# The prompt's delta rule rewritten: unrolled chunks, k and v turned inside the solve, v's rows added by a second product, the gated norm taken in by token

## The reference, cut to what matters

```python
A = where(strict, (k * beta) @ k.T * decay, 0)          # per head and chunk
sol = triangular_solve(A + I, concat([v * beta, k * beta * exp(gc)]))
u, w = sol[..., :DV], sol[..., DV:]
att = (q @ k.T) * decay
v_new = u - w @ S                                       # chunk after chunk
o = (q * exp(gc)) @ S + att @ v_new
S = S * exp(g_last) + (k * exp(g_last - gc)).T @ v_new
...
o = o * rsqrt(mean(o * o, -1) + eps) * norm_g * silu(z) # the gated norm
y = o @ w_out                                           # the output projection
```

## Time and profile before

| | us |
|---|---|
| median of 3 runs | 1880.82 (1878.73 to 1885.23) |
| the profiled execution | 1885.57 |
| its span | 1883.7 |
| PE busy | 1806.7 (96%) |
| DVE busy | 1158.7 (62%) |
| ACT busy | 461.0 (24%) |
| POOL busy | 258.8 (14%) |
| mean granted clock of PE, as a share of 2.4 GHz | 0.979 |

### The profile page before, as it was taken

How to read it: one execution, slowest core, us unless ns; L and a number is a source line. 1 busy time by engine, 2 the same in 40 slices (tenths; PEclk the granted TensorE clock), 3 DMA queues, 4 the chain that set the end, 5 groups by cost and what they waited for, 6 DMA issues and landing times. The chain is left out here.

```text
span 1883.7 us, 22711 instructions
## 1 busy us (share of the span) xinstructions
PE 1806.7 (96%) x7821; PEld 1400.7 (74%) x7821; DVE 1158.7 (62%) x2236; ACT 461.0 (24%) x1069; POOL 258.8 (14%) x554
## 2 busy tenths in 40 slices
PE   7999999999898999999999999998899999999999
PEld 4777677898476777777777777776577777777767
DVE  3756577675867666666243665547766666653365
ACT  1433412652213222222001311011322222200041
POOL 0111002326032000000011100001410000001120
PEclk9999999997999999999999999999899999999999
DMA  4111111002411222224113022210122222332111
GB/s 164 68 68 67 64 34 45 1 9 92 156 45 35 78 79 79 79 79 154 62 62 124 0 109 71 99 68 24 45 90 67 86 72 81 105 112 93 68 57 51
DMA packets 44455, 138.48 MB, mean 74 GB/s; under 512 B 4792, under 2 KB 12088, under 8 KB 44224
## 3 DMA queue, kind: packets, MB, share of 16 engines
q1 hardware_dynamic: 41648, 133.42, 20.4%
...
## 5 line engine op out<-in xcount | busy, mean ns | idle before, releaser
L267 PE MATMUL bank<-z,ring 128*128 128x288 f32 x1952 | 513.4, 410 | 6.3 <-DVE z L365 3.4
L267 PEld LDWEIGHTS bank<-z,ring 128*128 128x128 f32 x1952 | 374.3, 192 | 114.7 <-issue 4.1
L267 PE MATMUL bank<-x,ring 128*128 128x288 f32 x1632 | 429.9, 411 | 10.4 <-DMA x<-in_x 6.4
L267 PEld LDWEIGHTS bank<-x,ring 128*128 128x128 f32 x1632 | 312.5, 192 | 102.8 <-issue 13.7
L1946 DVE SCALAR_TENSOR_TENSOR scratch<-scratch 128x592 f32<-128x592 f32 x176 | 146.2, 831 | 25.8 <-ACT scratch L1890 24.1
L267 PE MATMUL bank<-y,ring 128*128 128x288 f32 x616 | 156.6, 406 | 1.0 <-ACT z L2010 0.5
L267 PE MATMUL bank<-big,ring 128*128 128x288 f32 x536 | 136.5, 410 | 6.0 <-issue 5.0
L267 PEld LDWEIGHTS bank<-y,ring 128*128 128x128 f32 x616 | 116.8, 190 | 34.1 <-ACT z L2010 1.0
L267 PEld LDWEIGHTS bank<-big,ring 128*128 128x128 f32 x536 | 102.2, 192 | 36.4 <-issue 7.3
L1890 ACT ACTIVATE scratch<-scratch 128x592 f32<-128x592 f32 x88 | 69.4, 789 | 91.2 <-DVE scratch L1920 89.5
L1980 POOL COPY scratch<-scratch 128x2 f32<-128x2 f32 x88 | 26.3, 299 | 464.1 <-ACT scratch L1876 464.1
...
## 6 DMA issues: line engine op xcount, KB each, us to landing
...
```

The lines of the kernel that those rows point to most:

```text
L267: last = pe.matmul(bank[:, 0:HALF], w[:, k * P:(k + 1) * P], rhs(k), start=start and k == 0, stop=k == self.depth - 1, skip_group_check=no ...
```

## The change

The loop becomes a class `Prompt` whose four chunks are written out. Decays and T have two buffers each, so the next chunk's are made during this one; the first ones are made in the front block. There is no staging tile. k and v are turned behind the first products of the two levels, and ACT copies v scaled by beta and k scaled by the last column of the decay. ACT also takes the right side out of the bank with a scale, and PE adds v's rows by a second product into the same sum. The output is made by token: ACT copies it to OT and squares it with a sum over the columns; POOL turns the sums into 1/rms (by a power of -0.5) and multiplies; PE turns the rows back behind the next chunk's new values, and DVE gates them into BIG. The last chunk's part of that stands in the samples' block, where POOL also makes the identities. `GatedNorm` becomes `SampleNorm`, for the samples' 64 columns only, and the output projection no longer waits for a norm of the prompt.

```diff
+DEC = [scratch(9216, H, CH), scratch(0, H, CH)]
+T_INV = [scratch(5120, H, 2, CH), scratch(1024, H, 2, CH)]
+KA, YS = scratch(3072, H, 2, CH), scratch(7168, H, CH)
+KTOK, VTOK, VNEW, EG = (scratch(at, H, P) for at in (8192, 10240, 11264, 12288))
+SS, RMS = CV[:, 112:120], CV[:, 120:128]
+def first_arg_pool(pool):
+    pool.wait_ge(gc_out, H)
+    pool.wait_ge(g_dve, 7)
+    pool.wait_ge(late_in, 64)
+    pool.tensor_tensor(DEC[0], Y[:, :, 0:CH], MASKT[:].unsqueeze(1).to_broadcast([P, H, CH]), ALU.add
+                       ).then_inc(dec_arg0, 1)
+def first_decay_act(act):
+    act.wait_ge(dec_arg0, 1)
+    act.wait_ge(tok_copied, 5)
+    for h in range(H):
+        act.activation(DEC[0][:, h, :], DEC[0][:, h, :], ACT.Exp, bias=TOKS[:, 0, 0, h:h + 1])
+def normalise(pool, nth, rms, scaled):
+    pool.tensor_scalar(RMS, SS, 1.0 / P, 1e-6, ALU.mult, ALU.add).then_inc(rms, 1)
+    pool.wait_ge(rms, 2 * nth + 1)
+    pool.tensor_tensor(RMS, RMS, NEG_HALF.to_broadcast([P, H]), ALU.pow).then_inc(rms, 1)
+    pool.wait_ge(rms, 2 * nth + 2)
+    pool.tensor_tensor(OT, OT, RMS.unsqueeze(2).to_broadcast([P, H, P]), ALU.mult).then_inc(scaled, 1)
+def gate_rows_dve(dve, c, h, gated):
+    cols = slice(c * CH, (c + 1) * CH)
+    dve.scalar_tensor_tensor(out=BIG[:, 3 * h + 1, cols], in0=BANK[h][:, 0:P], scalar=norm_g,
+                             in1=Z[:, h, cols], op0=ALU.mult, op1=ALU.mult).then_inc(gated, 1)
+class Prompt:
...
+    def pe(self, pe):
+        for c in range(NCH):
+            cols, T = self.col(c), T_INV[c % 2]
+            n, n2 = c * H + 1, 2 * c * H + 1
+            for h in range(H):
+                if c:
+                    pe.wait_ge(self.o_sq, n - H + h)
+                pe.matmul(BANK[h][:, 0:256], BIG[:, 3 * h, cols], BIG[:, 3 * h:3 * h + 2, cols], start=True,
+                          stop=True).then_inc(self.kq, 1)
+            pe.wait_ge(self.inited, NBL * (c + 1))
+            for h in range(H):
+                pe.wait_ge(self.att, n + h)
+                pe.matmul(BANK[h][:, 0:CH], KA[:, h, 0, :], T[:, h, 0, :], start=True, stop=True)
+                pe.transpose(BANK[h][:, CH:2 * CH], BIG[:, 3 * h + 2, cols], IDENT[:]).then_inc(self.y, 1)
+            for h in range(H):
+                pe.wait_ge(self.vtok, n + h)
+                pe.matmul(BANK[h][:, 256:384], T[:, h, 1, :], YS[:, h, :], start=True, stop=True)
+                pe.matmul(BANK[h][:, 384:512], YS[:, h, :], T[:, h, 1, :], start=True,
+                          stop=True).then_inc(self.d, 1)
+            for h in range(H):
+                pe.wait_ge(self.t, n + h)
+                pe.matmul(BANK[h][:, 0:CH], KA[:, h, 0, :], T[:, h, 0, :], start=True, stop=True)
+                pe.transpose(BANK[h][:, CH:2 * CH], BIG[:, 3 * h, cols], IDENT[:]).then_inc(self.y, 1)
+            for h in range(H):
+                pe.wait_ge(self.ktok, n + h)
+                pe.matmul(BANK[h][:, 384:512], YS[:, h, :], T[:, h, 1, :], start=True, stop=True)
+                pe.matmul(BANK[h][:, 0:P], BIG[:, 3 * h, cols], S[:, h, :], start=True,
+                          stop=True).then_inc(self.ks, 1)
+            if c:
+                pe.wait_ge(self.scaled, c)
+            for h in range(H):
+                pe.wait_ge(self.r, n + h)
+                pe.matmul(BANK[h][:, 128:256], T[:, h, 1, :], VTOK[:, h, :], start=True, stop=False)
+                last = pe.matmul(BANK[h][:, 128:256], T[:, h, 1, :], VNEW[:, h, :], start=False, stop=True)
+                if c:
+                    last = pe.transpose(BANK[h][:, 0:P], OT[:, h, :], IDENT[:])
+                last.then_inc(self.v, 1)
+            pe.wait_ge(self.qe, c + 1)
+            for h in range(H):
+                pe.wait_ge(self.vnew, n + h)
+                if c:
+                    pe.wait_ge(self.gated, n - H + h)
+                pe.matmul(BANK[h][:, 256:384], QE[:, h, :], S[:, h, :], start=True, stop=False)
+                pe.matmul(BANK[h][:, 256:384], KA[:, h, 1, :], VNEW[:, h, :], start=False, stop=True)
+                pe.matmul(BANK[h][:, 384:512], KTOK[:, h, :], VNEW[:, h, :], start=True,
+                          stop=True).then_inc(self.os, 1)
+    def dve(self, dve):
+        for c in range(NCH):
+            dec, T = DEC[c % 2], T_INV[c % 2]
+            n, n2 = c * H + 1, 2 * c * H + 1
+            for h in range(H):
+                if c:
+                    dve.wait_ge(self.dec, n - H + h)
+                dve.wait_ge(self.kq, n + h)
+                dve.tensor_tensor(KA[:, h], BANK[h][:, 0:256].rearrange("p (a b) -> p a b", a=2),
+                                  dec[:, h, :].unsqueeze(1).to_broadcast([P, 2, CH]),
+                                  ALU.mult).then_inc(self.att, 1)
+            for lv in range(LEVELS):
+                for h in range(H):
+                    dve.wait_ge(self.y, n2 + lv * H + h)
+                    dve.scalar_tensor_tensor(out=YS[:, h, :], in0=BANK[h][:, 0:CH],
+                                             scalar=TOKS[:, c, 1, h:h + 1], in1=MASKL[:, SAMP_LEVELS + lv, :],
+                                             op0=ALU.mult, op1=ALU.mult).then_inc(self.ymask, 1)
+                if lv == 0:
+                    for h in range(H):
+                        dve.wait_ge(self.d, n + h)
+                        dve.tensor_tensor(T[:, h], T[:, h],
+                                          BANK[h][:, 256:512].rearrange("p (a b) -> p a b", b=CH),
+                                          ALU.subtract).then_inc(self.t, 1)
+            for h in range(H):
+                dve.wait_ge(self.ks, n + h)
+                dve.tensor_tensor(T[:, h, 1, :], T[:, h, 1, :], BANK[h][:, 384:512],
+                                  ALU.subtract).then_inc(self.t1, 1)
+            if c:
+                for h in range(H):
+                    dve.wait_ge(self.vnew, n + h)
+                    gate_rows_dve(dve, c - 1, h, self.gated)
+            for h in range(H):
+                dve.wait_ge(self.os, n + h)
+                dve.scalar_tensor_tensor(out=S[:, h, :], in0=S[:, h, :], scalar=EG[:, h, CH - 1:CH],
+                                         in1=BANK[h][:, 384:512], op0=ALU.mult,
+                                         op1=ALU.add).then_inc(self.s_out, 1)
+    def inits(self, eng, c, some):
+        for r in some:
+            part = slice(BL * r, BL * (r + 1))
+            out = T_INV[c % 2][part, :, :, part].rearrange("p h a t -> p a t h")
+            eng(out, TD[part, :, :, c * H:(c + 1) * H]).then_inc(self.inited, 1)
+    def act(self, act):
+        self.inits(lambda out, x: act.activation(out, x, ACT.Copy), 0, (2, 3))
+        for c in range(NCH):
+            dec = DEC[c % 2]
+            n, n2 = c * H + 1, 2 * c * H + 1
+            act.activation(EG, Y[:, :, self.col(c)], ACT.Exp).then_inc(self.eg, 1)
+            for h in range(H):
+                act.wait_ge(self.ymask, n2 + h)
+                act.activation(VTOK[:, h, :], BANK[h][:, CH:2 * CH], ACT.Copy,
+                               scale=TOKS[:, c, 1, h:h + 1]).then_inc(self.vtok, 1)
+            if c + 1 < NCH:
+                act.wait_ge(self.arg, c + 1)
+                for h in range(H):
+                    act.activation(DEC[1 - c % 2][:, h, :], DEC[1 - c % 2][:, h, :], ACT.Exp,
+                                   bias=TOKS[:, c + 1, 0, h:h + 1]).then_inc(self.dec, 1)
+            for h in range(H):
+                act.wait_ge(self.ymask, n2 + H + h)
+                act.activation(KTOK[:, h, :], BANK[h][:, CH:2 * CH], ACT.Copy,
+                               scale=dec[:, h, CH - 1:CH]).then_inc(self.ktok, 1)
+            for h in range(H):
+                act.wait_ge(self.t1, n + h)
+                act.activation(VNEW[:, h, :], BANK[h][:, 0:P], ACT.Copy,
+                               scale=TOKS[:, c, 2, h:h + 1]).then_inc(self.r, 1)
+            for h in range(H):
+                act.wait_ge(self.v, n + h)
+                act.activation(VNEW[:, h, :], BANK[h][:, 128:256], ACT.Copy).then_inc(self.vnew, 1)
+            for h in range(H):
+                act.wait_ge(self.s_out, n + h)
+                act.activation(OT[:, h, :], BANK[h][:, 256:384], ACT.Copy)
+                act.activation(Y[:, h, self.col(c)], BANK[h][:, 256:384], ACT.Square,
+                               accum_out=SS[:, h:h + 1]).then_inc(self.o_sq, 1)
+    def pool(self, pool):
+        self.inits(pool.tensor_copy, 0, (0, 1))
+        pool.wait_ge(self.inited, NBL)
+        for c in range(NCH):
+            if c:
+                pool.wait_ge(self.o_sq, c * H)
+                normalise(pool, c - 1, self.rms, self.scaled)
+            pool.wait_ge(self.eg, c + 1)
+            pool.tensor_tensor(QE, BIG[:, 1:QKV_T:3, self.col(c)], EG, ALU.mult).then_inc(self.qe, 1)
+            if c + 1 < NCH:
+                pool.tensor_tensor(DEC[1 - c % 2], Y[:, :, self.col(c + 1)],
+                                   MASKT[:].unsqueeze(1).to_broadcast([P, H, CH]), ALU.add
```

(48 more changed lines are left out.)

303 lines of the change are left out of this document (54 added, 249 removed).

## The result

The changed kernel takes **1859.1 us**, the median of 4 runs (1857.8 to 1864.29), against 1880.86 (1878.73 to 1885.23) of the kernel before, run beside it: a ratio of 0.9887, 95% interval 0.9861 to 0.9912. Forecast was 1860.2, range 1851 to 1869.

A forecast was written before the change was run, and what follows sets the result against it. PE was taken as nearly the bound in the prompt's rule. 10.0 - 1.0 + 12.8 - 1.2 = 20.6 us off the profiled 1885.57; with the profile 4.75 above the median 1880.82, forecast 1860.2 us, range 1851 to 1869.

The forecast's parts named there:

- the four terms: Forecast changes by stretch: prompt's rule 10.0 us gained, sample block 1.0 lost, gated norm 12.8 gained, front 1.2 lost.
- a clock dip of 1.7: Last block: PE standing nearly 4 us in one piece lowers the clock, costing 1.7 of the 14.5 us gain.
- The count: Prompt's rule: PE's instructions per chunk sum to 25.8 us, the first chunk 24.9, four chunks 102.2.
- The stall: Prompt's rule: PE waits 0.5 us before the third solve step in two chunks, 1.0 in all, for POOL's late argument.
- The pair on ACT: Prompt's output step: one head's copy plus summing square on ACT costs 0.6 to 0.9 us.
- The rival on POOL: Prompt's rule: power takes 3 to 5 us, stalls of 2 to 4 twice, kernel 1863 to 1867; chance 0.22.
- The rival in which POOL makes the kernel slower: Prompt's rule: gain gone at an 11.5 us power; at 16, stalls of 30 us and kernel 1893; chance 0.05.
- whichever of the two goes first, the other is late: Sample block: POOL's identity copy (some 2.4 us) and DVE's arguments take turns, so moving the copy gains 0.
- gates 0.8, transposes 0: Sample block: first gate delays PE's state products by 0.8 us; the eight transposes fall between DVE's last subtractions.
- The rival in which the block stays at full clock: Sample block: denser prompt keeps PE's clock, likely 5 us back, kernel 1855; chance 0.12.
- the wait of nearly 4 us in one piece: Last block: PE stands 6 of its first 18.7 us, nearly 4 in one piece, waiting for DVE's token work.
- The collision: Front: POOL's first decay argument and DVE's four operations take turns; DVE loses 2.35 us, about 1.2 reach PE.

The follow-up runs named there:

- the run with the argument first: Changed kernel, but POOL makes the next chunk's decay argument before normalising the chunk before; 1854.63 us, ratio 0.9859 to the kernel before.
- the line through 8 and 512 columns: Changed kernel with POOL's power on 512 columns in the last block, replacing root and reciprocal: 1932.85 us; that power took 81.96 us, against 1.66 for 8 columns.
- four of the variants: Edits of the changed kernel: decay argument before norm, 1854.63 us; first decay argument later, 1854.40; 28 transposes before the prompt's first product, 1865.05; four edits together, 1839.20.

## Why the prediction was right, and where it wasn't

**Total.** 1860.2 against 1859.1. Its terms add up to 20.6, those of the profile to 24.5 (27.7 less the 3.24 in unchanged code), and the medians show 21.8. The total is right to within what executions differ by, and that it is right to 1.1 is in part luck: the four terms missed by 0, +2.3, +0.9 and +0.6 us, all to one side, and the two profiles stand differently to their medians (4.75 above, 1.3 below). The two large terms were right in their mechanism (the norm's but for a clock dip of 1.7); the sample block's had the wrong sign, and the front's twice the size.

**The prompt's rule: 10.0 forecast, 10.04 measured.** The count held: 25.8 for PE and a stall make 26.12 a chunk, 103.07 from the block's start to the end of the last product, forecast 103.2. PE as the bound is shown by the run with the right side on DVE (16 instructions a chunk, 1.79 each time). The stall came to 0.77 in all (the run with the argument first), forecast 1.0: the power took 1.66 instead of 1.5, but the multiply 1.90 instead of 2.36. The pair on ACT, put at 0.6 to 0.9, takes 0.53. The rival on POOL had its place right and its price too low: 2 us per us late is the wait alone, and waits over 3 us add 1.6 of half clock each. The rival in which POOL makes the kernel slower would need, by the line through 8 and 512 columns, the power on some 70 columns rather than 8. The first power came without a load ahead of it; the Trainium skill (GPSIMD Engine Reference, 2.1 Instruction dispatch) speaks of about 6 us for a freshly loaded routine, and no row here shows one.

**The sample block: -1.0 forecast, +1.31 measured.** The step that failed is "whichever of the two goes first, the other is late", taken as the whole story of the copy. POOL's copy took 1.03, not 2.4, and delayed DVE's arguments by 0.8; the solve still started 1.8 us earlier than before, because POOL's clearing was no longer beside DVE's copy. I had read 2.66 as the copy's own price without asking what POOL ran at 424. The second step that failed: gates 0.8, transposes 0. It was gates 0, transposes 1.76. So the 1.8 won at the start went to the transposes, and the two cancel in the measurement. What is left, 1.3, is mostly clock, which the forecast had set apart: the state products took 11.56 for 13.59, and a spell at 452 (5.37 us) gave part of it back. The rival in which the block stays at full clock didn't come in this profile (0.50 in the solve); it came in four of the variants'.

The Trainium skill (SBUF — State Buffer, Who interferes with whom) also says that a copy on DVE can take both port pairs, and that of DVE and GpSimd the one that issues second then blocks for the whole instruction. The rows agree on whole-instruction waiting, with DVE's copy as the one that waits: 2.66 beside POOL's clearing and 0.68 without it, 1.83 and 0.17.

**The gated norm: 12.8 forecast, 13.68 measured.** PE was forecast to go on behind its wait 18.7 us into the block and did at 18.9, released by DVE; the wait of nearly 4 us in one piece was 3.66. The clock dip of 1.7 didn't come: the window of that wait is at 1.00, and the 32 products behind it took 8.00 us, where 32 took 7.92 before. Of the resulting 14.3, 0.6 was lost later.

**The front: -1.2 forecast, -0.57 measured.** The collision came as read: DVE lost 1.96 and POOL 1.7, forecast 2.35 in all for DVE. PE waited 0.51 for it.
